# A two-block transformer kernel on one core: load queues, ring timing, projection banks, head norm and the expert layer's entry wait changed

## The reference

```
for i in range(DEPTH):
    shift, scale, gate = split(silu(c) @ ada_w[i] + ada_b[i], 3)
    h = rms_norm(x, norm_g[i]) * (1 + scale) + shift
    x = x + gate * mixer(h)
```

## Time and profile before

| | us |
|---|---|
| median of 3 runs (1480.57 to 1482.54) | 1481.17 |
| the profiled execution, its own time | 1483.22 |
| its span, first to last instruction | 1481.6 |

### The profile page before, as it was taken

The page is one execution under the profiler, slowest core; times in us unless marked ns, Lnnn a source line. Parts: engine busy times, 40 slices in busy tenths (PEclk is TensorE's granted clock), DMA queues, the critical chain, the costliest instruction groups (busy, mean ns, idle before and its releaser), DMA issues.

```text
span 1481.6 us, 22247 instructions
## 1 busy us (share of the span) xinstructions
PE 1328.3 (90%) x8323; PEld 1136.9 (77%) x8323; DVE 1068.1 (72%) x2301; ACT 589.9 (40%) x1096; POOL 272.0 (18%) x199
## 2 busy tenths in 40 slices
PE   4877889868795889886999999999999999999997
PEld 4556765557465855886999999999997888888886
DVE  5577687765765684699990788888987666766676
ACT  0333476223622253343555444444444333333332
POOL 0332101241030002363999200000000000000000
PEclk9989899998897988997999999999999999999999
DMA  9566732476237811513445344444446555555552
GB/s 351 204 203 225 269 111 72 171 257 230 80 135 256 305 37 41 216 58 121 160 173 185 138 148 143 143 151 150 143 171 198 186 187 188 192 185 185 189 193 100
DMA packets 101183, 253.69 MB, mean 171 GB/s; under 512 B 9432, under 2 KB 16856, under 8 KB 100704
## 3 DMA queue, kind: packets, MB, share of 16 engines
q1 hardware_dynamic: 76368, 204.31, 39.3%
q10 hardware_dynamic: 24720, 48.11, 9.7%
HBM read 251.34 MB, written 1.05 MB: 170 GB/s over the span
## 4 chain that ended last, share of the span: by engine, by line
PE 65%; DVE 16%; issue 5%; DMA 5%; POOL 5%; ACT 3%; SPq 1%; ACTq 0%; POOLq 0%; DVEq 0%
PE bank L1581 24%; PE bank L1573 18%; PE bank L631 6%; PE bank L1855 4%; DMA arena<-in_w_ada 3%; PE bank L1025 3%; DVE arena L425 3%; PE bank L732 2%; POOL u_lo L1613 2%; DMA arena<-in_ada_w 2%; DVE v_lo L623 1%; PE bank L844 1%; PE bank L935 1%; POOL head_ms L753 1%; POOL v_lo L1613 1%
## 5 line engine op out<-in xcount | busy, mean ns | idle before, releaser
L1573 PE MATMUL bank<-h_hi,u_hi 128*128 128x256 f32 x624 | 181.2, 290 | 18.7 <-DVE arena L1766 17.3
L1573 PE MATMUL bank<-h_lo,u_hi 128*128 128x256 f32 x624 | 177.4, 284 | 0.0
L1573 PE MATMUL bank<-h_hi,u_lo 128*128 128x256 f32 x624 | 177.4, 284 | 0.0
L425 DVE SCALAR_TENSOR_TENSOR arena<-arena,silu_c 128x512 f32<-128x512 f32 x154 | 118.7, 771 | 54.2 <-DMA arena<-in_w_ada 34.3
L1573 PEld LDWEIGHTS bank<-h_hi,u_hi 128*128 128x128 f32 x624 | 120.6, 193 | 19.0 <-issue 17.5
L1573 PEld LDWEIGHTS bank<-h_lo,u_hi 128*128 128x128 f32 x624 | 120.7, 193 | 0.0
L1573 PEld LDWEIGHTS bank<-h_hi,u_lo 128*128 128x128 f32 x624 | 120.4, 193 | 0.0
L2037 POOL TENSOR_SCALAR stat<-stat 128x1 f32<-128x1 f32 x2 | 0.4, 190 | 647.8 <-ACT arena L2034 647.8
L1573 PE MATMUL bank<-h_hi,v_hi 128*128 128x256 f32 x400 | 115.5, 289 | 1.7 <-POOL v_lo L1613 1.7
L1573 PE MATMUL bank<-h_hi,v_lo 128*128 128x256 f32 x400 | 113.1, 283 | 0.0
L1573 PE MATMUL bank<-h_lo,v_hi 128*128 128x256 f32 x400 | 113.1, 283 | 0.0
(11 more groups left out here) (272 smaller groups left out, 3546.7 us busy)
## 6 DMA issues: line engine op xcount, KB each, us to landing
raw<-in_u SPq DMA_DIRECT2D x128, 512.0 KB, 3.5
raw<-in_v SPq DMA_DIRECT2D x128, 512.0 KB, 3.5
arena<-in_w_ada ACTq DMA_DIRECT2D x96, 256.0 KB, 3.5
arena<-in_ada_w ACTq DMA_DIRECT2D x64, 256.0 KB, 3.3
raw<-in_nsa_w_in SPq DMA_DIRECT2D x4, 2048.0 KB, 8.8
arena<-in_moba_w_in SPq DMA_DIRECT2D x4, 2048.0 KB, 10.7
arena<-in_ada_w SPq DMA_DIRECT2D x12, 512.0 KB, 11.6
arena<-in_w_in SPq DMA_DIRECT2D x3, 2048.0 KB, 11.4
```

Source lines behind the costliest of these rows:

```text
L425: m = V.did(ve.scalar_tensor_tensor(out=acc, in0=src, scalar=factor, in1=acc, op0=ALU.mult, op1=ALU.add))
L1573: last = pe.matmul(zbank[k].t[:, 0:S], u[:, c, :], h[:, c, :], start=n == 0, stop=n == 3 * DC - 1)
```

## The change

- `ask_chunks` issues on SyncE instead of ScalarE, and always up to four buffers ahead. Bias rows move to SyncE as well.
- Weight tiles become objects declared ahead of the layers; their loads are issued by ScalarE (`load_all`) at places written by hand, mostly after the first tile or column block of the projection two tiles earlier. The first three go on SyncE. The gate weights get a buffer of their own.
- The start: tile 0 first, then quarters of tiles 3, 1 and 2 together, x and the row constants on SyncE between and behind them; tiles 1 and 2 are multiplied by one instruction of 128 x 1024 per chunk; the transposes of h go ahead of the last sums.
- `proj_bank` takes turns between banks 0, 1, 6 and 7.
- `head_norm` is cut in two; `trickle` runs between the halves, with 2 steps where there were 3, and 1 where there were 2. The bank is freed after the second half. `project_cols` spends 2 for 3.
- The transposes of h multiply x by a diagonal matrix of the reciprocal root mean square, so that the product on VectorE falls away. The second token tile is turned inside the first projection's matmuls.
- Low halves of some tiles (z1, out1, qb, kb, vb) go to VectorE and GpSimd in turn.
- The four engines before the expert loop no longer wait for `V.last()`. `FIRST_Z` is 40 instead of 44. The weights of both token tiles are computed first, then come two lead blocks, both transposes, and two lead blocks. `V_ORDER` follows from the new slots.

```diff
-FIRST_Z = 44
+FIRST_Z = 40
...
-        b = banks[turn["proj"] % 2]
+        b = banks[(0, 1, 6, 7)[turn["proj"] % 4]]
...
+    def load_all(tiles):
+
+        for tile in tiles:
+            tile.load(A)
...
-        while chunk_count["asked"] < min(len(chunk_order), chunk_count["used"] + CHUNKS - spare):
+        while chunk_count["asked"] < min(len(chunk_order), chunk_count["used"] + CHUNKS):
...
-            A.need(chunk_free[i])
-            chunk_mark[i] = chunk_load[i].did(ac.dma_start(chunk_buf[i], src[c * P:(c + 1) * P, j * WT:(j + 1) * WT]))
+            Y.need(chunk_free[i])
+            chunk_mark[i] = chunk_load[i].did(sy.dma_start(chunk_buf[i], src[c * P:(c + 1) * P, j * WT:(j + 1) * WT]))
...
+                src = arena[:, 0:2 * DC * WT].rearrange("p (r c n) -> p r c n", r=2, c=DC)[:, :, c, :]
+                V.need(first_mark[1][q], first_mark[2][q])
...
-                last = pe.transpose(b.t[:, i * P:(i + 1) * P], src[:, c * P:(c + 1) * P], ident[:])
-            b.free = put(half, b.t, T.did(last))
-            out.append(b.free)
+                last = pe.matmul(b.t[:, i * P:(i + 1) * P], src[:, c * P:(c + 1) * P], diagonal, start=True, stop=True)
+            out.append((b, T.did(last)))
...
-            m_xn[t] = V.did(ve.tensor_scalar(xn[t], x[:, t, :], stat[:, t:t + 1], None, ALU.mult))
+            m_diag[t] = V.did(ve.tensor_scalar(diagonal[t], ident[:], stat[:, t:t + 1], None, ALU.mult))
...
+    def settle_use(b, second, steps):
+
+        trickle(steps)
+        b.free = second() if callable(second) else second
...
+                if first_tile and (t, c) == (0, 5):
+                    second_tile_turn()
...
-            b.free = use(t, b.t[:], m)
-            trickle(3)
+            settle_use(b, use(t, b.t[:], m), 2)
+            if t == 0:
+                load_all(loads)
...
+            m_power = head_power(ps, 8, tmp[:], buf_free(t, m))
+
+            def second():
+                m_src, mq = head_norm(ps, qn[:], 8, tab_g, t, HD ** -0.5, tmp[:], m_power)
...
+        project_split(q0, q_tile_use(qT, 0, row("nsa_q_norm"), qbufs), cmp0, (w1_tiles[0],))
+        cmp_inputs(0, cmp0, kv1, (cmp1,))
+        project_split(kv1, kv_use(1), cmp1, (q1,))
...
-            e.need(*h_split, T.last(), A.last(), V.last())
+            e.need(*h_split, T.last(), A.last())
...
-            for k in range(2):
-                lead_block(FIRST_Z + 2 * t + k)
+            m_w[t] = V.did(ve.tensor_tensor(hk[:, t, 2], weight[:, t], gsum.unsqueeze(2).broadcast_to([P, PH, PTOP]), ALU.mult))
+        for k in range(2):
+            lead_block(FIRST_Z + k)
...
+        for k in range(2, LEAD):
+            lead_block(FIRST_Z + k)
...
-    V_ORDER = (3, 0, 1, 2)
+    V_ORDER = (3, 1, 2, 0)
```

More of the change, by code:

```diff
@@ L486, in first_products, with first_bias @@
                                  skip_group_check=True)
-        first_sum[j] = T.did(last)
+        return T.did(last)
+    def first_bias(which, at, n, m):
+        b = first_banks[which]
+        V.need(m, m_cols)
+        b.free = V.did(ve.tensor_tensor(ada[0][:, at:at + n], b.t[:, 0:n], col("ada_b", 0, 24)[:, at:at + n], ALU.add))
+        for j in range(at // 4, (at + n) // 4):
+            ada_mark[0, j] = b.free
     current = []
     def trickle(n):
-        if fillers or current:
-            ask_chunks()
         while n > 0:
@@ L715, in project_cols_split, with project_cols_by_tile @@
             trickle(2)
-    def project_cols_by_tile(tile, use, ahead=None):
-        w, m_w, slot = tile
+            if i == 0:
+                load_all(loads)
+    def project_cols_by_tile(tile, use, ahead=None, loads=()):
+        w = tile.w
         pair = [proj_bank() for _ in range(2)]
-        T.need(pair[0].free, pair[1].free, m_w)
+        T.need(pair[0].free, pair[1].free, tile.mark)
         for t in range(NT):
-            if h_mark[t] is None:
-                second_turn[0].run()
-                split_h(1, V)
-                if ahead:
-                    ahead.step(4)
             T.need(*h_mark[t])
@@ L734, in project_cols_by_tile, with head_power @@
             pe_us[0] += 7.2
-        slot_free[slot] = [m := T.did(last)]
+            if t == 0 and ahead:
+                ahead.step(4)
+        slot_free[tile.slot] = [m := T.did(last)]
         for i in range(WT // P):
             pair[i // 2].free = use(i, pair[i // 2].t[:, (i % 2) * S:(i % 2 + 1) * S], m)
+        load_all(loads)
         trickle(8)
     hn = sb("head_ms", [P, NH])
-    def head_norm(src, dst, n, g, tab, post, tmp, marks, g_heads=None):
-        s3, d3, t3 = (v.rearrange("p (h d) -> p h d", d=HD) for v in (src, dst, tmp))
-        np_ = src.shape[0]
+    def head_power(src, n, tmp, marks):
+        t3, np_ = tmp.rearrange("p (h d) -> p h d", d=HD), src.shape[0]
         A.need(*marks)
@@ L827, in kv_tile_use @@
+            return second
         return use
@@ L995, in times_z, with gated_out @@
         return done
-    def gated_out(w_src, layer, stack, begin_next, turn_next, rstd=None):
+    def gated_out(first, second, layer, stack, begin_next, turn_next, place_next, loads, rstd=None):
         gate = 1 if layer == 1 else 0
@@ L1022, in gated_out @@
                 b = proj_bank()
-                T.need(b.free, m_w, *oz_mark[t])
+                T.need(b.free, first.mark, *oz_mark[t])
                 for c in cs:
-                    last = pe.matmul(b.t[:], hT[:, c, t * P:(t + 1) * P], w[:, c, :], start=c == cs[0], stop=c == cs[-1])
-                slot_free[slot] = [m := T.did(last)]
+                    last = pe.matmul(b.t[:], hT[:, c, t * P:(t + 1) * P], first.w[:, c, :], start=c == cs[0],
+                                     stop=c == cs[-1])
+                slot_free[first.slot] = [m := T.did(last)]
                 add_rows(0, t, n, b, m)
```

444 lines of the change are left out of this document (243 added, 201 removed).

## The result

| | before | after |
|---|---|---|
| median of 4 runs, us | 1480.87 | 1428.39 (1424.85 to 1429.53) |
| profiled execution, own time, us | 1483.22 | 1428.41 |
| its span, us | 1481.6 | 1427.1 |

The ratio is 0.9642 [0.9621, 0.9662]: 52.5 us faster, where 77 were forecast. The time lies in the range that was given; the likeliest case does not hold as it was argued.

The account below looks back on a forecast made before the run. TensorE is full from 829.6 us; before that, transfers bound the start and waits in turn the projection stages. -7.4 - 9 - 44 + 2 - 18.4 = -76.8 from 1483.2, less 2.0: 1404 us, range 1370 to 1438.

Parts of the forecast that it names:

- the likeliest case: Whole kernel: the prediction's own sum of terms, -76.8 us, giving 1404 us; chance 0.52.
- The start: Before the first projection: quarters land earlier and it starts at 34.6 instead of 42.1 us; -7.4, between -4 and -9.
- Turning h: Transposes of h before projections and queries: waits for ScalarE's columns and L567 go, diagonal products cost like transposes; -9 us.
- The projection stages: Three layers' projections: four banks, early chunks, split head norm and fewer steps remove waits (36) and raise the clock (8); -44 us.
- `ensure`: Output stages of layers 1 and 2: 98 and 148 steps done before 96 and 144 are asked, so none is forced.
- Attention of layer 2: Seven more modulation steps on VectorE fall into this stage; +2 us, between 0 and +5.3.
- The expert layer: Entry wait -16.5, first block -2.3, gates -1.6, against +2 for a search late by 1.6 us; sum -18.4 us.
- A: Rival, projection stages: transfers, not the asking queue, are full; -15 instead of -44, giving 1433 us; chance 0.18.
- B: Rival, projection stages: all waits and half the clock's shortfall go; -75 instead of -44, giving 1373 us; chance 0.15.
- C: Rival, expert loop's entry: the wait only changes its name; -76.8 without the 16.5, giving 1421 us; chance 0.08.
- D: Rival, expert layer: GpSimd's splits slow the whole search, TensorE stands for 104 us, giving 1506 us; chance 0.03.
- The other signs: First projection at 34 to 36 us; entry wait under 2; `in_w_ada` waits below 10; no L1126/L1062 waits; clock 0.93+.

Follow-up runs that it names:

- Experiment 2: The changed kernel, but h is turned by transposes of the normalised tile instead of products with a diagonal: 1426.29 us, ratio 0.9621 to the kernel before.
- experiment 12: The changed kernel with pending sums first in `ensure`, transposes, ten low halves on VectorE, and also the low half of h's first tile on VectorE: 1398.95 us.
- experiment 7: The changed kernel with queues exchanged: chunks (all four buffers) and bias rows issued by ScalarE, weight tiles by SyncE: 1449.32 us, ratio 0.9795.
- experiment 10: The changed kernel, but VectorE again makes the ten low halves that the change gave to GpSimd: 1422.15 us, ratio 0.9594.
- experiment 1: The changed kernel, but `ensure` first runs pending sums and forces eight more steps only if a column is still missing: 1421.27 us, ratio 0.9587.
- experiment 3: The changed kernel, with VectorE's last instruction waited for again at the entry of the expert loop: 1446.16 us, ratio 0.9746.
- experiments 5 to 7: The first of these: the changed kernel, chunks and bias rows again from ScalarE, two buffers kept back, weight tiles staying with ScalarE: 1461.71 us, ratio 0.9868.
- experiment 6: The changed kernel, but weight tiles are issued from SyncE's queue, among the chunks that stay there: 1457.80 us, ratio 0.9817.

## Why the prediction came out as it did

**The start**, -7.4 forecast, -4.9 measured. The last quarter came at 29.1 instead of 28.2 us; the 128x1024 step took 1.30 us each, 2.6 in all for 2.9. The forecast put the transposes ahead of the sums at no cost, but as products they took 3.54 us there (1.95 before), until 33.4. VectorE's last step was done at 31.7, and the 16 columns of sums could go only behind the products, from 33.2 to 35.1. The first projection then waited 2.16 us for ScalarE's columns. Experiment 2 has it at 36.8.

**Turning h**, -9 forecast, +2.5 measured (the stretches before the first split product of layers 0 and 1, the projections of layer 2 and the queries, -0.7 + 0.5 + 1.3 + 0.4, and 1 us ahead of the scores). This step failed, at the sentence that the product with a diagonal "has the form of the transposes, and I cost it at the same": 2.02 us for 1.09, eight times. It failed at a second place too: "the second by the product that falls away". The diagonal that took the product's place is short only where GpSimd is idle, 0.28 us; at the second turns it took 2.35, held by GpSimd's low half of h (experiment 12), and TensorE waited 5.1 us for it in three times. L567's three waits were 3.5. The other half of the forecast came true and did not help: the 6.8 us of waits for ScalarE's columns are gone, and these waits and 7.4 us of longer products stand in their place. With both causes removed, experiments 2 and 12 give back 2.1 and 8.8 us.

**The projection stages**, -44 forecast, -51.4 measured: the size is right within its ends, the reasons are partly other ones. Early chunks and four banks were said to bring it; two banks cost only 4.5 us, keeping two buffers back nothing. The norm's two parts are 5.0. The largest part that the runs show, 20.9 us, is one that the working did not have: it read TensorE's and VectorE's waits and not ScalarE's, and so did not see 43 us in which ScalarE, with the high halves behind it, waited for a free chunk buffer (experiment 7, with its reservation). These three come to 30.4 us if they add up. The other 21 of the 51.4 are shown by no run: the fewer steps and the earlier tiles were not tried apart. The low halves were counted as relief for VectorE, "less these steps and the low halves that go to GpSimd"; experiment 10 shows them as a cost of 6.2 us. The clock gave more than the 8 us taken. Over the three stretches of the landmark table TensorE was busy for 224.2 of 288.7 us before and for 205.7 of 237.3 now, with 1343 and 1335 matmul records. So 33.0 us are idle time that went, where 36 were taken, and 18.4 us are mostly matmuls that ran shorter, at granted clocks of 0.94, 0.94 and 0.97 for 0.89, 0.88 and 0.86.

**`ensure`**. "By counting calls, 98 steps are done before layer 1's output stage asks for 96 ... so `ensure` is never made to do them at once" failed. The stretch is 12.9 us longer, the largest miss; experiment 1 takes away 10.6 of them, 7.1 of the whole, and 2.3 stay open. The count was right (`ensure` found 98 steps done); that a column counts as done only when its sum has been issued was left out. Against the span's -54.5 the sum of -76.8 is off by 22.3. These 12.9 and the 11.5 of the turn are 24.4; the start and the small stretches cost 6.0 more than forecast, the stages and the expert layer gave 8.1 more.

**Attention of layer 2**, +2 forecast, +3.1 measured, for the reason given: more steps in it.

**The expert layer**, -18.4 forecast, -19.1 measured. The entry is exact (-16.0 of -16.5; experiment 3 gives it back, +17.8). But the search was not late by 1.6 us. VectorE still waited 11.5 us for the exponential (34.6 before), 1.7 of them its own time, so 9.8 us were to spare. L1768 of the earlier trace rows is L1859 now:

```profile
L1859 DVE TENSOR_TENSOR arena<-arena x2: 2292/3336/4381, 644.3 to 692.6; 128x2048 f32<-128x2048 f32 x2
```

The forecast added 2.1 us to the first of them, since GpSimd would now work beside it. That one took 2.29 us as before: VectorE had started at 644.26, and it was GpSimd, from 645.65, that took 5.54 us for two halves where two others took 4.77. The search's second half came down from 101.3 to 95.6 us. So the price goes to whoever starts second. Not every instruction of VectorE's pays it: the search's MAX8 on 128x128 at 639.66 us took 0.30 us inside GpSimd's halves of 639.30 to 644.07. The Trainium skill (SBUF — State Buffer, section SBUF: two separate sides) has the two engines share ports as a lock held for a whole instruction by the one that starts first. The trace agrees here and in experiments 10 and 12 (0.25 to 2.30 us, 0.28 to 2.36).

**The rivals.** A (chunks stay late, 1433) gives the nearest time, and that is luck: it has 15 us from the stages, which gave 51.4. Its sign is not as clear as it was meant to be. The waits for `in_w_ada` fell from 34.3 to 15.1 us, below its 25 but above the forecast's 10; with `in_ada_w`, which the prediction left out of its "34.3 us ... for modulation chunks", they are 26.1 of 47.0. A leaned on the Trainium skill (DMA: Bandwidth & Descriptors, section Issuing engines are not separate DMA queues), which has the transfers of all issuing engines run on the same DMA engines. That fits: the DMA share was 1.00 in layer 2's stage with two engines issuing, and 104.8 to 104.9 MB moved from 40 us to the expert loop in each of experiments 5 to 7. The same section has issue from several engines save only the sequencer's time. Here chunks and tiles from SyncE alone, instead of from two engines, cost 29.4 us more (experiment 6). No run shows how much of that is SyncE's wait for a slot, 24.7 us, and how much the landing behind a tile, 13.2 us for 7.3. What stands behind the asking engine had a price of its own, 20.9 us (experiment 7). B, C and D did not come: the stages kept waits, the entry wait went, the search had 9.8 us to spare.

**The other signs.** The entry wait (1.2 us), the bank waits that are gone and the clock of the three stages are as forecast. The first projection at 37.2 us (34 to 36) and the waits for `in_w_ada` are not.

## What to carry to other kernels

Before a load is moved to another engine, read the waits of the engine that issues: what it has queued behind a wait for a free buffer is the real price of a load, and it shows up two engines further on. That can be compute, as ScalarE's high halves here, or other loads, as the chunks behind a tile's slot. Small transfers that are needed soon went better from another engine than the large ones. Work handed to GpSimd was no relief for VectorE: a half of 2.4 us there cost VectorE 2.0 where they met, against 1.22 for doing it. And a test for "done" in a planner must tell work that is missing from work that only waits to be issued.

## What the runs showed of the hardware that was not expected

- Issued by the same engine right behind a 2 MB tile, a chunk of 256 KB landed after 13.2 us, as late as the tile (12.9). Issued by another engine than the tiles it landed after 7.3 us (median of 24), at 372 GB/s and a DMA share of 1.00.
- Where VectorE's instruction was held by GpSimd's subtraction of 128x1024 (2.3 to 2.4 us), its own length did not matter: two on 128x8 went from 0.25 to 2.30 us, one on 128x128 from 0.28 to 2.36, one on 128x1024 from 0.75 to 2.83.
- An fp32 product with a 128x128 diagonal shows two records for each: eight take 2.02 us, where eight transposes take 1.09.
